# Output projection of the last two chunks split in two, and two expert matrices loaded at other times

## Chip, cores and metric

One core of one Trainium2 chip runs the whole program. The metric is the time of one execution in microseconds of device time (us), as the median of several runs. TensorE (PE) multiplies matrices into PSUM, VectorE (DVE), ScalarE (ACT) and GpSimd (POOL) work on rows, and SyncE (SP) issues most transfers (DMA) and computes nothing.

## What is computed

The reference is one layer of a streaming encoder for 560 tokens of width 1024 (16 meta tokens, 512 of a prompt, 32 of running streams), all in float32. The parts that matter here:

```
h = rmsnorm(x, g_mix); proj = h @ w_in                       # GLU halves, q, k, v
a_out = silu(layernorm(causal_dwconv(u_hist, conv_w, conv_b)))   # group A, 512 channels
b_out = head_rmsnorm(stick_breaking(q, k_all, v_all, q_start))   # group B, 512 channels
x = x + jnp.concatenate([a_out, b_out], axis=-1) @ w_out     # w_out is 1024 x 1024
x = x + hier_moe(rmsnorm(x, g_ffn), ...)                     # top 2 of 32 experts per token
...
gu = hf @ w_e_in[e]                                          # 1024 x 512 for each expert
act = silu(gu[:, :256]) * gu[:, 256:]
out = out + gates[:, e:e + 1] * (act @ w_e_out[e])           # 256 x 1024 for each expert
```

The weights of the 32 experts are 32 times 2 MB (`w_e_in`) and 32 times 1 MB (`w_e_out`).

## The kernel before

Tokens are held in five chunks: four of 128 rows and a last one of 64 (`ROWS`). The engines' programs are written out by hand, each in a fixed order, and meet at semaphores (`wait_ge`, `then_inc`); nothing is scheduled by a tool.

**First half.** Input projection, convolution, attention. Their outputs stand in `mixt`: `k` 0 to 3 is the convolution's half of the channels, `k` 4 to 7 is attention's. `w_out` lies in the tile `cw` (all 8192 columns; columns 4096 to 8191 are its rows for `k` 4 to 7).

**The middle**, which the change touches. For each chunk `c`, PE's `project(c, ks, ns)` multiplies `mixt` by `wout` into the PSUM banks `OUT_BANK[c]`; `LATE` is the order (4, 5, 6, 7, 0, 1, 2, 3) of `k`. DVE's `residual(c)` waits for `res_done` and adds the result to `x`; ACT and DVE make the second norm (`normed_h2`, `h2_ready`); SP stores it to memory (`h2_dram`) for the experts' gathers; PE turns it (`turn_h2`) and makes the router's scores (`logits`); DVE picks two experts for each token (`choose`, `picks_ready`); PE counts positions (`positions`, which waits for `picks_ready`); DVE and PE make a table of rows (`place_at`, `places`, `entries`, `table`). From that table GpSimd gathers the first rows.

**Last half.** 16 pairs of experts. For a pair `g`, PE runs `gate_up(g)`, `turn(g + 1)`, `turn_act(g)`, `down(g)`. Weights lie in 7 slots for `w_e_in` (`WI_SLOTS`) and 7 for `w_e_out`; expert `e` uses slot `e % 7`. SP loads expert 7 and 8's `w_e_in` only after `gu_done` of pair 0, since they take the slots of experts 0 and 1, expert 7's `w_e_out` after `y_done` of pair 0, and so on: from there each load waits for the slot that PE frees. Slot 6 of `w_e_in` is `cw[:, 4096:8192]`, the place of `w_out`'s second half. Slot 5 is made of pieces of the tile `low` (`wi5`) that hold the second norm's rows and the router's data until the gather.

SP's order around the change is the whole of this:

```
            load_one_wo(1)
            for c in range(NC):
                if c == 4:
                    sp.wait_ge(res_done, NC)
                    load_wi(4)
                sp.wait_ge(h2_ready, c + 1)
                sp.dma_start(h2_dram[...], h2[c % 2][...])
            load_wi(6)
            sp.wait_ge(logit_done, NC)
            ...
            sp.wait_ge(gathered[0], 16)
            load_wi(5)
            load_one_wo(4)
            sp.wait_ge(ent_ready, 1)
            load_one_wo(6)
```

Of the kernel before, what the change touches and what calls it, by code (L numbers as in the profile page):

```python
# [11 lines left out]
ALU = mybir.AluOpType  # L12
# [8 lines left out]
P = 128  # L21
# [3 lines left out]
NI = CC // P  # L25
# [8 lines left out]
ROWS = [P, P, P, P, COLS - 4 * P]  # L34
# [13 lines left out]
WI_SLOTS, WO_SLOTS, ROW_BUFS = 7, 7, 1  # L48
# [17 lines left out]
def build(nc, x_prompt, x_sample, cache_k, cache_v, cache_conv, meta, g_mix, w_in, conv_w, conv_b,  # L66
          ln_g, ln_b, g_sb, w_out, g_ffn, w_rg, b_rg, w_re, b_re, w_ei, w_eo, g_fin,
          y_p, y_s, nk_p, nv_p, ncv_p, nk_s, nv_s, ncv_s):
    with ExitStack() as ctx:
# [9 lines left out]
        x = sb("x", [P, NC, D])  # L79
# [78 lines left out]
        def two(lo):  # L158
# [17 lines left out]

        wi = [t.rearrange("p (k n) -> p k n", k=KD)
              for t in [slots[q][:, 0:4096] for q in (2, 3, 0, 1, 4, 5)] + [cw[:, 4096:8192]]]
        wi5 = [(slice(0, 6), lowf[:, 9216:12288].rearrange("p (k n) -> p k n", k=6)),
               (slice(6, KD), lowf[:, 6144:7168].rearrange("p (k n) -> p k n", k=2))]  # L180

        def wi_at(e, k):

            if e % WI_SLOTS == 5:
                return wi5[k // 6][1][:, k % 6, :]
            return wi[e % WI_SLOTS][:, k, :]

        wo = [t.rearrange("p (k n) -> p k n", k=2)
# [255 lines left out]
            return CHUNK_OF.index(c) + 1  # L444

        OUT_BANK = (4, 2, 6, 2, 6)
        MEAN_BANK, LN_BANK = 2, 0

        acc = ps[:, 6:8, :].rearrange("p b n -> p (b n)")[:, 0:CW]
        shared = [(0, j) for j in range(SHARED_FROM, TAPS)] + [(1, j) for j in range(TAPS)]  # L450
# [33 lines left out]
        def _(sp):  # L484
# [112 lines left out]
            load_wi(1)  # L597
            sp.wait_ge(small_stored, 16 * 8)
            load_one_wo(1)
            for c in range(NC):  # L600
                if c == 4:
                    sp.wait_ge(res_done, NC)
                    load_wi(4)
                sp.wait_ge(h2_ready, c + 1)
                sp.dma_start(h2_dram[P * c:P * c + ROWS[c], :], h2[c % 2][0:ROWS[c], :]).then_inc(h2_stored[c % 2], 16)
            load_wi(6)
            sp.wait_ge(logit_done, NC)
            sp.wait_ge(h2_stored[0], 16 * 3)
            sp.wait_ge(h2_stored[1], 16 * 2)
            sp.wait_ge(gsub_ready, 3)  # L610
            sp.wait_ge(gathered[0], 16)
            load_wi(5)
            load_one_wo(4)
            sp.wait_ge(ent_ready, 1)
            load_one_wo(6)
# [259 lines left out]
        def _(pe):  # L875
# [266 lines left out]

            LATE = (4, 5, 6, 7, 0, 1, 2, 3)

            def project(c, ks, ns=(0, 1)):
                w = ROWS[c]

                def ready(k):
                    if k < NI and c == 0:
                        pe.wait_ge(mixa_ready, k + 1)  # L1150
                    elif k == NI:
                        pe.wait_ge(mixb_ready, mixed(c))

                if w < P:
                    for k in ks:
                        for n in ns:
                            mm = pe.matmul(ps[w * n:w * n + w, OUT_BANK[c] + n, :], mixt[:, k, P * c:P * c + w],
                                           wout[:, k, 512 * n:512 * n + 512], start=k == LATE[0], stop=k == LATE[-1],
                                           skip_group_check=True)
                    mm.then_inc(res_done, 1)  # L1160
                    return
                for n in ns:
                    for k in ks:
                        if n == ns[0]:
                            ready(k)
                        mm = pe.matmul(ps[0:w, OUT_BANK[c] + n, :], mixt[:, k, P * c:P * c + w],  # L1166
                                       wout[:, k, 512 * n:512 * n + 512], start=k == LATE[0], stop=k == LATE[-1],
                                       skip_group_check=True)
                if ks[-1] == LATE[-1] and ns[-1] == 1:
                    mm.then_inc(res_done, 1)  # L1170
# [36 lines left out]
            def turn_h2(c):  # L1207
                w = ROWS[c]
                pe.wait_ge(h2_ready, c + 1)
                if c >= 1:  # L1210
                    pe.wait_ge(h2t_ready, c)
                else:
                    pe.wait_ge(co_ready, 2)
                pt = ps[:, 0:2, :].rearrange("p b (k t) -> p (b k) t", t=P)
                for k in range(KD):
                    mm = pe.transpose(pt[:, k, 0:w], h2[c % 2][0:w, P * k:P * k + P], ident[0:w, 0:w])
                    if c == NC - 1 and k == KD // 2 - 1:
                        mm.then_inc(h2_turned, 1)
                mm.then_inc(h2_turned, 1)

            def logits(c):

                if c == 0:
                    pe.wait_ge(router_loaded, 16 * 5)
                if c >= 2:
                    pe.wait_ge(at_ready, c - 1)
                w = ROWS[c]
                pe.wait_ge(h2t_ready, c + 1)
                for k in range(KD):
                    if c == NC - 1 and k == KD // 2:  # L1230
                        pe.wait_ge(h2t_ready, NC + 1)
                    mm = pe.matmul(ps[0:w, 4 + c % 2, 0:36], h2t[c % 2][:, k, 0:w], wrt[:, k, :],
                                   start=k == 0, stop=k == KD - 1, skip_group_check=True)
                mm.then_inc(logit_done, 1)
# [51 lines left out]

            turn_co()
            project(0, LATE[4:])
            project(1, LATE[4:])
            turn_h2(0)  # L1290
            project(2, LATE[4:], (0,))
# [2 lines left out]
            turn_h2(1)  # L1294
            project(2, LATE[4:], (1,))
            logits(1)
            project(3, LATE, (0,))
            turn_h2(2)
            positions(0)
            project(3, LATE, (1,))  # L1300
            positions(1)
            logits(2)
            pe.wait_ge(x2_ready, 3)
            project(4, LATE)
            turn_h2(3)
            positions(2)
            pe.wait_ge(x2_ready, 4)
# [23 lines left out]

            def gate_up(g):
                for e in (2 * g, 2 * g + 1):
                    pe.wait_ge(wi_loaded[e % WI_SLOTS], (e // WI_SLOTS * 16 + 16) * (2 if e % WI_SLOTS == 5 else 1))
                pe.wait_ge(xt_ready, g + 1)
                if g == 2:
                    pe.wait_ge(tab_ready, 2)
# [402 lines left out]
        def _(dve):  # L1740
# [3 lines left out]
            def halves(t):  # L1744
                return t.rearrange("p (a t) -> p a t", a=2)
# [300 lines left out]
            def residual(c):  # L2046

                w = ROWS[c]
                dve.wait_ge(res_done, c + 1)
                if w == P:  # L2050
                    dve.tensor_tensor(x[0:w, c, :].rearrange("p (a n) -> p a n", a=2), x[0:w, c, :].rearrange("p (a n) -> p a n", a=2),
                                      ps[0:w, OUT_BANK[c]:OUT_BANK[c] + 2, :], ALU.add).then_inc(x2_ready, 1)
                else:
                    for n in range(2):
                        cols = slice(512 * n, 512 * n + 512)
                        dve.tensor_tensor(x[0:w, c, cols], x[0:w, c, cols], ps[w * n:w * n + w, OUT_BANK[c] + n, :], ALU.add).then_inc(x2_ready, 1)

            def normed_h2(c):
# [23 lines left out]
                rooted[0] += 1  # L2082
                dve.wait_ge(rstd_ready, rooted[0])
                dve.tensor_scalar(h, h, stat[0:w, 32 + c:33 + c], None, ALU.mult).then_inc(h2_ready, 1)

            def choose(c):

# [51 lines left out]
            link(dve.tensor_scalar(low2.rearrange("p c k f -> p c (k f)"), wide(colid, 4), -BIGF, None, ALU.add))  # L2139
            link(dve.tensor_scalar(low2[:, :, 1, 1], low2[:, :, 1, 1], float(COLS), None, ALU.add))  # L2140
            normed_h2(0)
            residual(1)
            normed_h2(1)
            residual(2)
# [195 lines left out]
```

## Time and profile before

| | |
|---|---|
| median of 3 runs | 561.22 us (561.11 to 561.43) |
| the profiled execution's own time | 562.51 us |
| its span, first to last instruction | 560.8 us |
| PE busy | 507.7 us (91%) |
| DVE, ACT, POOL busy | 267.4, 165.8, 146.3 us |
| mean granted TensorE clock | 0.97 |
| moved by DMA | 148.93 MB, mean 266 GB/s |

The profile is of one execution. Its own time is 1.7 us more than its span (what lies before the first and after the last instruction) and 1.3 us over the median. PE is busy in most of the span, but a share over the whole span says little here: the DMA engines move 420 GB/s in the last 40% of the span and 2 GB/s in some stretches before it.

### The profile page before, as it was taken

Reading aid. Unit: us, or ns where it says so; the run is one execution under the profiler, and the core shown is the slowest. Engines: PE = TensorE matmul, PEld = TensorE weight load, DVE = VectorE, ACT = ScalarE, POOL = GpSimd, SP = SyncE. Lnnn points to the kernel's source line nnn. Section 1 sums busy time; section 2 is a strip of 40 time slices with the busy share of each in tenths; the row PEclk is TensorE's granted clock in tenths of the full one; section 3 lists DMA queues with packets and bytes.
Section 4 is the critical chain, followed back from the end, with each engine's and each line's share of the span. In section 5 each row is a group of like instructions: output and inputs, shape, how many; then the busy total and the mean of one; then the engine's idle time right before and its main releaser. Section 6 shows DMA issues by size and latency. Waiting matters only on the chain.

```text
span 560.8 us, 7885 instructions
## 1 busy us (share of the span) xinstructions
PE 507.7 (91%) x3147; PEld 320.5 (57%) x3148; DVE 267.4 (48%) x471; ACT 165.8 (30%) x280; POOL 146.3 (26%) x143
## 2 busy tenths in 40 slices
PE   5999999999979889999997999999999678798993
PEld 5679999999847567545556634344434223333330
DVE  1870788999578897225668422111111111111157
ACT  4422555554476784032112011111111110111122
POOL 3002699998210102101021202111211110111003
PEclk9999999999979999999996899999999998999997
DMA  8902855500523602599117799999999999999994
GB/s 290 246 12 61 279 158 175 195 0 1 196 76 122 226 1 49 203 429 406 58 56 302 272 415 425 421 428 419 422 421 420 425 426 424 423 418 421 393 345 164
DMA packets 44763, 148.93 MB, mean 266 GB/s; under 512 B 7124, under 2 KB 23532, under 8 KB 36279
## 3 DMA queue, kind: packets, MB, share of 16 engines
q1 hardware_dynamic: 40263, 139.63, 64.3%
q0 software_dynamic: 4464, 8.80, 4.2%
q8 instruction: 25, 0.41, 0.3%
q14 instruction: 11, 0.09, 0.1%
HBM read 136.29 MB, written 19.59 MB: 278 GB/s over the span
## 4 chain that ended last, share of the span: by engine, by line
PE 61%; DMA 20%; DVE 9%; issue 4%; SPq 4%; ACT 1%; POOL 1%; DVEq 0%; POOLq 0%; ACTq 0%
PE ps L949 18%; DMA big<-in_w_expert_out 13%; PE ps L1166 10%; PE ps L1348 9%; PE ps L1373 5%; DMA cw<-h_dram,low 4%; PE ps L914 3%; DVE ps L1928 3%; SPq L628 2%; PE ps L1069 2%; PE ps L1329 2%; DMA y_dram<-cw,low 1%; PE ps L1017 1%; DMA big<-y_dram 1%; PE ps L902 1%
## 5 line engine op out<-in xcount | busy, mean ns | idle before, releaser
L2230 DVE TENSOR_TENSOR low<-low,ps 128x256 f32<-128x256 f32 x16 | 6.7, 422 | 173.2 <-ACT low L1700 173.2
L1348 PE MATMUL ps<-big,low 128*64 128x512 f32 x320 | 85.0, 593 | 3.7 <-issue 2.3
L949 PE MATMUL ps<-cw_r 128*128 128x280 f32 x256 | 72.3, 292 | 0.0
L949 PE MATMUL ps<-low_r,cw_r 128*128 128x280 f32 x256 | 72.2, 292 | 0.0
L949 PE MATMUL ps<-cw_r,big_r 128*128 128x280 f32 x256 | 72.1, 291 | 0.0
L1851 DVE SCALAR_TENSOR_TENSOR ps<-low,cwt,ps 128x590 f32<-128x590 f32 x80 | 66.9, 837 | 2.8
L1373 PE MATMUL ps<-big,low 128*64 128x512 f32 x160 | 46.9, 629 | 11.5 <-DMA big<-in_w_expert_out 4.6
L1166 PE MATMUL ps<-cw,low 128*128 128x512 f32 x128 | 56.6, 595 | 0.0
L1348 PEld LDWEIGHTS ps<-big,low 128*64 128x64 f32 x320 | 29.8, 137 | 46.0 <-issue 45.9
L734 POOL TENSOR_TENSOR big<-big 128x590 f32<-128x590 f32 x36 | 46.9, 1304 | 3.3
L949 PEld LDWEIGHTS ps<-cw_r 128*128 128x128 f32 x256 | 47.2, 188 | 0.4 <-issue 0.4
L949 PEld LDWEIGHTS ps<-cw_r,big_r 128*128 128x128 f32 x256 | 47.3, 188 | 0.0
L949 PEld LDWEIGHTS ps<-low_r,cw_r 128*128 128x128 f32 x256 | 47.2, 188 | 0.0
L1711 ACT ACTIVATE cw<-ps,low 128x1024 f32<-128x1024 f32 x16 | 17.8, 1115 | 98.1 <-PE ps L1373 98.1
L1348 PE MATMUL ps<-low 128*64 128x512 f32 x128 | 42.3, 593 | 0.2 <-issue 0.2
L814 POOL DMA_INDIRECT y_dram<-cw,low x15 | 15.1, 1009 | 101.7 <-ACT cw L1711 96.6
L802 POOL DMA_INDIRECT cw<-h_dram,low x16 | 16.6, 1035 | 94.1 <-PE ps L1329 82.5
L1166 PEld LDWEIGHTS ps<-cw,low 128*128 128x128 f32 x128 | 23.7, 190 | 26.8 <-issue 26.8
L1700 ACT ACTIVATE low<-ps 128x256 f32<-128x256 f32 x16 | 6.2, 384 | 108.5 <-PE ps L1348 108.5
L712 POOL TENSOR_TENSOR stat<-stat,nhalf 128x1 f32<-128x1 f32 (+2 forms) x16 | 15.3, 957 | 83.9 <-DVE stat L2075 32.6
L724 POOL TENSOR_TENSOR big_r<-big,cw_r 128x1024 fp32r<-128x1024 f32 x13 | 31.2, 2400 | 11.6 <-ACT cw_r L1494 11.6
L1373 PEld LDWEIGHTS ps<-big,low 128*64 128x64 f32 x160 | 14.8, 144 | 31.3 <-issue 31.3
(274 smaller groups left out, 816.7 us busy)
## 6 DMA issues: line engine op xcount, KB each, us to landing
big<-in_w_expert_in SPq DMA_DIRECT2D x16, 2048.0 KB, 20.6
big<-in_w_expert_out SPq DMA_DIRECT2D x20, 1024.0 KB, 26.1
big<-in_w_in SPq DMA_DIRECT2D x20, 512.0 KB, 5.3
low<-in_w_expert_out SPq DMA_DIRECT2D x8, 1024.0 KB, 31.5
low<-in_w_expert_in SPq DMA_DIRECT2D x4, 2048.0 KB, 23.3
cw<-in_w_expert_in SPq DMA_DIRECT2D x4, 2048.0 KB, 27.2
low<-in_w_expert_in SPq DMA_DIRECT2D x4, 1536.0 KB, 22.5
big<-in_w_expert_in SPq DMA_DIRECT2D x6, 1024.0 KB, 32.4
```

What stands on the lines that cost most here:

```text
L712: pool.tensor_tensor(t, t, nhalf[0:t.shape[0], :].broadcast_to(list(t.shape)), ALU.pow).then_inc(rstd_ready, 1)
L724: pool.tensor_tensor(w_lo[j % WSLOTS], win[j % WSLOTS], w_hi[j % HSLOTS].bitcast(F32), ALU.subtract).then_inc(w_lo_ready, 1)
L734: pool.tensor_tensor(conv[:, i, :], t, conv[:, i, :], ALU.add).then_inc(pool_tap_done, 1)
L802: pool.indirect_dma_start(out=xg_of(g), out_offset=None, in_=h2_dram, in_offset=bass.IndirectOffsetOnAxis(ap=rows_of[:, g, 0:1].bitcast(U3 ...
L914: mm = pe.matmul(ps[:, 4 + c % 2, :], h[:, k, cols], wts[:, k, :], start=m == 0 and k == 0, stop=m == 2 and k == KD - 1, skip_group_check= ...
L949: return pe.matmul(ps[:, proj_bank(j) + half, 0:PROJ], w[:, k, :], h[:, k, cols], start=first, stop=last, skip_group_check=True)
L1166: mm = pe.matmul(ps[0:w, OUT_BANK[c] + n, :], mixt[:, k, P * c:P * c + w], wout[:, k, 512 * n:512 * n + 512], start=k == LATE[0], stop=k = ...
L1348: mm = pe.matmul(ps[TILE * half:TILE * half + TILE, gu_bank(g), :], xt[:, k, TILE * half:TILE * half + TILE], wi_at(2 * g + half, k), star ...
L1373: mm = pe.matmul(ps[TILE * half:TILE * half + TILE, 4 + m, :], gact_t[:, k, TILE * half:TILE * half + TILE], wo[(2 * g + half) % WO_SLOTS] ...
L1711: act.activation((yg_end if g == PAIRS - 1 else yg[b]).rearrange("p (m n) -> p m n", m=2), ps[:, 4:6, :], ACT.Copy, scale=tab[:, g, 2:3]). ...
L1851: ins = dve.scalar_tensor_tensor(acc, src, w, acc, ALU.mult, ALU.add)
L1928: dve.tensor_tensor_scan(k, k, nones[:, 0:1].broadcast_to([P, n]), carry[:, a:a + 1] if cached else 1.0, ALU.mult, ALU.max).then_inc(left_ ...
```

## The change

PE gets `project_late(c)` for chunks 3 and 4. It multiplies attention's half (`k` 4 to 7) of these chunks into other banks (`LATE_BANK`), right behind chunk 0's projection; DVE's `residual_late(c)` adds that to `x`, and the later `project(3)` and `project(4)` take `k` 0 to 3 alone. The second half of `w_out` is then read for the last time much earlier in PE's order, and SP issues expert 6's `w_e_in` into its place before the stores of the second norm, where it stood behind them. `wi5` becomes three pieces; two of them (6 of 8 `k`, 1.5 MB) are loaded as soon as the router's scores and the stores are done, and the third where the whole stood, behind the gather.

```
-        wi5 = [(slice(0, 6), lowf[:, 9216:12288].rearrange("p (k n) -> p k n", k=6)),
+        wi5 = [(slice(0, 4), lowf[:, 9216:11264].rearrange("p (k n) -> p k n", k=4)),
+               (slice(4, 6), lowf[:, 11264:12288].rearrange("p (k n) -> p k n", k=2)),
                (slice(6, KD), lowf[:, 6144:7168].rearrange("p (k n) -> p k n", k=2))]
...
-        MEAN_BANK, LN_BANK = 2, 0
+        MEAN_BANK, LN_BANK, LATE_BANK = 2, 0, {3: 0, 4: 4}
...
             load_one_wo(1)
+            sp.wait_ge(mean_done, 3)
+            load_wi(6)
             for c in range(NC):
...
-            load_wi(6)
             sp.wait_ge(logit_done, NC)
             sp.wait_ge(h2_stored[0], 16 * 3)
             sp.wait_ge(h2_stored[1], 16 * 2)
+
+            def load_first_wi5(n):
+                ks, dst = wi5[n]
+                sp.dma_start(dst, w_ei[0, 5].rearrange("(p k) n -> p k n", p=P)[:, ks]).then_inc(wi_loaded[5], 16)
+
+            load_first_wi5(0)
+            load_first_wi5(2)
             sp.wait_ge(gsub_ready, 3)
             sp.wait_ge(gathered[0], 16)
-            load_wi(5)
+            load_first_wi5(1)
             load_one_wo(4)
...
+            def project_late(c):
+
+                w = ROWS[c]
+                if c == 3:
+                    pe.wait_ge(co_ready, 2)
+                else:
+                    pe.wait_ge(x2_ready, 1)
+                for k in LATE[0:4]:
+                    for n in range(2):
+                        lo = w * n if w < P else 0
+                        mm = pe.matmul(ps[lo:lo + w, LATE_BANK[c] + n, :], mixt[:, k, P * c:P * c + w], wout[:, k, 512 * n:512 * n + 512],
+                                       start=k == LATE[0], stop=k == LATE[3], skip_group_check=True)
+                mm.then_inc(mean_done, 1)
...
-                    pe.wait_ge(co_ready, 2)
+                    pe.wait_ge(dev_ready, NI + 1)
...
             project(0, LATE[4:])
+            project_late(3)
+            project_late(4)
             project(1, LATE[4:])
...
-            project(3, LATE, (0,))
+            project(3, LATE[4:], (0,))
             turn_h2(2)
             positions(0)
-            project(3, LATE, (1,))
+            project(3, LATE[4:], (1,))
...
-            project(4, LATE)
+            project(4, LATE[4:])
...
+            def residual_late(c):
+
+                w = ROWS[c]
+                dve.wait_ge(mean_done, c - 1)
+                if w == P:
+                    dve.tensor_tensor(halves(x[0:w, c, :]), halves(x[0:w, c, :]), ps[0:w, LATE_BANK[c]:LATE_BANK[c] + 2, :],
+                                      ALU.add).then_inc(dev_ready, 1)
+                    return
...
             normed_h2(0)
+            residual_late(3)
+            residual_late(4)
             residual(1)
```

PE, from the projection of chunk 0 on (L1166 and in the changed file L1190 are `project` for whole chunks, L1216 and L1240 `turn_h2`, L1232 and L1257 `logits`). Before:

```order
L1139 MATMUL ps<-ident,low 30x128 x8
L1166 MATMUL ps<-cw,low 128x512 x16
L1216 MATMUL ps<-ident,low 128x128 x8
L1166 MATMUL ps<-cw,low 128x512 x4
L1232 MATMUL ps<-low 128x36 x8
```

The same place of the change:

```order
L1149 MATMUL ps<-ident,low 30x128 x8
L1190 MATMUL ps<-cw,low 128x512 x8
L1165 MATMUL ps<-cw,low 128x512 x8
L1165 MATMUL ps<-cw,low 64x512 x8
L1190 MATMUL ps<-cw,low 128x512 x8
L1240 MATMUL ps<-ident,low 128x128 x8
L1190 MATMUL ps<-cw,low 128x512 x4
L1257 MATMUL ps<-low 128x36 x8
```

Sixteen matmuls (L1165, eight of 128 rows and eight of 64) now stand between chunk 0's and chunk 1's projection.

PE, from the scores of chunk 1 to those of chunk 2 and the projection of chunk 4 (L1242 and L1267 are `positions`, L1157 and L1181 `project` of the chunk of 64 rows). Before:

```order
L1232 MATMUL ps<-low 128x36 x8
L1166 MATMUL ps<-cw,low 128x512 x8
L1216 MATMUL ps<-ident,low 128x128 x8
L1242 MATMUL ps<-low,tril 128x32
L1166 MATMUL ps<-cw,low 128x512 x8
L1242 MATMUL ps<-low,onesb 128x32
L1242 MATMUL ps<-low,tril 128x32
L1232 MATMUL ps<-low 128x36 x8
L1157 MATMUL ps<-cw,low 64x512 x16
L1216 MATMUL ps<-ident,low 128x128 x8
```

The same place of the change:

```order
L1257 MATMUL ps<-low 128x36 x8
L1190 MATMUL ps<-cw,low 128x512 x4
L1240 MATMUL ps<-ident,low 128x128 x8
L1267 MATMUL ps<-low,tril 128x32
L1190 MATMUL ps<-cw,low 128x512 x4
L1267 MATMUL ps<-low,onesb 128x32
L1267 MATMUL ps<-low,tril 128x32
L1257 MATMUL ps<-low 128x36 x8
L1181 MATMUL ps<-cw,low 64x512 x8
L1240 MATMUL ps<-ident,low 128x128 x8
```

The order is the same, with half as many matmuls ahead of `turn_h2(2)`, ahead of the end of chunk 3 and in chunk 4.

SP, from expert 1's `w_e_out` to the loads behind the gather, with what each waits for (L576 and L578 load a whole `w_e_in`, L574 and L616 pieces of expert 5's, L581 and L583 a `w_e_out`, L605 and L609 store the second norm). Before:

```order
L581 DMA big<-in_w_expert_out 128x2048 [waits small_stored]
L605 DMA h_dram<-low 128x1024 [waits h2_ready] x4
L576 DMA low<-in_w_expert_in 128x4096 [waits res_done]
L605 DMA h_dram<-low 64x1024 [waits h2_ready]
L576 DMA cw<-in_w_expert_in 128x4096
L574 DMA low<-in_w_expert_in 128x3072 [waits gsub_ready,h2_stored1,gathered0,h2_stored0,logit_done]
L574 DMA low<-in_w_expert_in 128x1024
L581 DMA low<-in_w_expert_out 128x2048
```

The same place of the change:

```order
L583 DMA big<-in_w_expert_out 128x2048 [waits small_stored]
L578 DMA cw<-in_w_expert_in 128x4096 [waits mean_done]
L609 DMA h_dram<-low 128x1024 [waits h2_ready] x4
L578 DMA low<-in_w_expert_in 128x4096 [waits res_done]
L609 DMA h_dram<-low 64x1024 [waits h2_ready]
L616 DMA low<-in_w_expert_in 128x2048 [waits h2_stored1,h2_stored0,logit_done]
L616 DMA low<-in_w_expert_in 128x1024
L616 DMA low<-in_w_expert_in 128x1024 [waits gathered0,gsub_ready]
L583 DMA low<-in_w_expert_out 128x2048
```

The load into `cw` (2 MB) has moved ahead of the five stores, and two of the three pieces of expert 5 (1.5 MB) stand ahead of the wait for the gather.

## Rows read from the trace of the kernel before

**Rows 1.** Windows: us, busy of each engine, PE clock, DMA share, GB/s.

```profile
270.00:280.00 10.00, 10.00 (x31) 4.92 (x30) 6.62 (x30) 1.01 (x1) 1.27 (x1) 1.00 0.13 52
280.00:290.00 10.00, 10.00 (x49) 4.95 (x49) 5.43 (x13) 1.15 (x2) 1.33 (x1) 1.00 0.01 2
308.00:310.00 2.00, 2.00 (x12) 2.00 (x11) 1.73 (x11) 0.70 (x1) 1.40 (x2) 0.50 0.01 4
311.90:322.00 10.10, 10.10 (x86) 5.43 (x86) 4.96 (x20) 0.00 (x0) 0.99 (x1) 0.99 0.90 335
322.00:531.00 209.00, 184.48 (x875) 76.49 (x875) 30.43 (x46) 22.48 (x30) 29.02 (x29) 0.98 1.01 421
```

**Rows 2.** Timeline of PE: start, us, line, records (two for a matmul).

```profile
242.91 13.90 PE L1166 MATMUL ps<-cw,low 128*128 128x512 f32 x32
257.52 3.60 PE L1166 MATMUL ps<-cw,low 128*128 128x512 f32 x8
260.96 1.87 PE L1232 MATMUL ps<-low 128*128 128x36 f32 x16
...
268.71 7.11 PE L1166 MATMUL ps<-cw,low 128*128 128x512 f32 x16
275.66 1.04 PE L1216 MATMUL ps<-ident,low 128*128 128x128 f32 x8
276.53 0.18 PE L1242 MATMUL ps<-low,tril 128*128 128x32 bf16 x1
...
285.45 7.09 PE L1157 MATMUL ps<-cw,low 128*64 128x512 f32 x32
292.47 1.09 PE L1216 MATMUL ps<-ident,low 128*128 128x128 f32 x8
```

**Rows 3.** Timeline of DVE, in brackets idle before and its releaser.

```profile
271.38 0.75 DVE L2084 TENSOR_SCALAR low<-low,stat 128x1024 f32<-128x1024 f32 x1 [0.52 <-POOL stat L712]
...
274.46 0.19 DVE L2104 TENSOR_TENSOR low<-negs 128x32 bf16<-128x32 f32 x1
...
283.78 1.22 DVE L2051 TENSOR_TENSOR x<-x,ps 128x1024 f32<-128x1024 f32 x1 [5.85 <-PE ps L1166]
...
291.68 0.19 DVE L2104 TENSOR_TENSOR low<-negs 128x32 bf16<-128x32 f32 x1
292.58 1.40 DVE L2056 TENSOR_TENSOR x<-x,ps 64x512 f32<-64x512 f32 x2 [0.71 <-PE ps L1157]
```

**Rows 4.** Timeline of SP: its DMA issues.

```profile
298.41 0.59 SPq L576 DMA_DIRECT2D cw<-in_w_expert_in  x1
311.88 0.80 SPq L574 DMA_DIRECT2D low<-in_w_expert_in  x2
312.72 0.43 SPq L581 DMA_DIRECT2D low<-in_w_expert_out  x1
319.29 0.33 SPq L581 DMA_DIRECT2D cw<-in_w_expert_out  x1
322.00 0.80 SPq L576 DMA_DIRECT2D big<-in_w_expert_in  x2
327.74 0.33 SPq L581 DMA_DIRECT2D big<-in_w_expert_out  x1
```

**Rows 5.** DMA issues at 292.58 and 319.29, us to landing; the page's software queue.

```profile
low<-in_w_expert_in SPq DMA_DIRECT2D x1, 2048.0 KB, 7.8
...
cw<-in_w_expert_out SPq DMA_DIRECT2D x1, 1024.0 KB, 7.7
...
q0 software_dynamic: 4464, 8.80, 4.2%
```

**Rows 6.** Windows of PE alone: us, busy, clock, DMA share, GB/s.

```profile
298.00:300.00 2.00, 1.70 (x19) 0.62 0.91 356
162.00:164.00 2.00, 1.18 (x16) 0.50 0.00 0
190.00:192.00 2.00, 0.78 (x4) 1.00 0.52 198
```

More of the change, by code:

```diff
@@ L184, in wi_at @@
             if e % WI_SLOTS == 5:
-                return wi5[k // 6][1][:, k % 6, :]
+                ks, t = wi5[(0, 0, 0, 0, 1, 1, 2, 2)[k]]
+                return t[:, k - ks.start, :]
             return wi[e % WI_SLOTS][:, k, :]
@@ L1143, in _ @@
             LATE = (4, 5, 6, 7, 0, 1, 2, 3)
+            def project_late(c):
[10 more added lines that the diff above has]
+                mm.then_inc(mean_done, 1)
             def project(c, ks, ns=(0, 1)):
-                w = ROWS[c]
+                w, first = ROWS[c], LATE[0 if c < 3 else 4]
                 def ready(k):
@@ L1157, in project @@
                             mm = pe.matmul(ps[w * n:w * n + w, OUT_BANK[c] + n, :], mixt[:, k, P * c:P * c + w],
-                                           wout[:, k, 512 * n:512 * n + 512], start=k == LATE[0], stop=k == LATE[-1],
+                                           wout[:, k, 512 * n:512 * n + 512], start=k == first, stop=k == LATE[-1],
                                            skip_group_check=True)
@@ L1166, in project @@
                         mm = pe.matmul(ps[0:w, OUT_BANK[c] + n, :], mixt[:, k, P * c:P * c + w],
-                                       wout[:, k, 512 * n:512 * n + 512], start=k == LATE[0], stop=k == LATE[-1],
+                                       wout[:, k, 512 * n:512 * n + 512], start=k == first, stop=k == LATE[-1],
                                        skip_group_check=True)
@@ L1224, in logits @@
                     pe.wait_ge(router_loaded, 16 * 5)
+                    pe.wait_ge(dev_ready, NI + 3)
                 if c >= 2:
@@ L1333, in gate_up @@
                 for e in (2 * g, 2 * g + 1):
-                    pe.wait_ge(wi_loaded[e % WI_SLOTS], (e // WI_SLOTS * 16 + 16) * (2 if e % WI_SLOTS == 5 else 1))
+                    pe.wait_ge(wi_loaded[e % WI_SLOTS], (e // WI_SLOTS * 16 + 16) * (len(wi5) if e % WI_SLOTS == 5 else 1))
                 pe.wait_ge(xt_ready, g + 1)
@@ L2050, in residual @@
                 if w == P:
+                    if c == 3:
+                        dve.wait_ge(dev_ready, NI + 1)
                     dve.tensor_tensor(x[0:w, c, :].rearrange("p (a n) -> p a n", a=2), x[0:w, c, :].rearrange("p (a n) -> p a n", a=2),
@@ L2053, in residual @@
                 else:
+                    dve.wait_ge(dev_ready, NI + 3)
                     for n in range(2):
@@ L2084, in normed_h2 @@
                 dve.tensor_scalar(h, h, stat[0:w, 32 + c:33 + c], None, ALU.mult).then_inc(h2_ready, 1)
+            def residual_late(c):
[5 more added lines that the diff above has]
+                    return
+                for n in range(2):
+                    cols = slice(512 * n, 512 * n + 512)
+                    dve.tensor_tensor(x[0:w, c, cols], x[0:w, c, cols], ps[w * n:w * n + w, LATE_BANK[c] + n, :],
+                                      ALU.add).then_inc(dev_ready, 1)
             def choose(c):
```

## The prediction

> **What bounds the kernel now.** I read the windows first, to find where the DMA engines work and where they rest. In 270 to 290 they move 52 and 2 GB/s, in 308 to 310 they move 4, and from 322 to 531 they hold 421 GB/s at a busy share of 1.01 [rows 1]. So the last half is bound by the weights: in those 209 us PE is busy 184.5, and it is PE that waits. The middle is another matter. There I read PE's timeline: from 242.91 to 293.56 (the end of the turn that starts at 292.47) PE has no pause, projection after projection [rows 2]. DVE waits for PE (5.85 us ahead of chunk 3's residual, 0.71 us ahead of chunk 4's) [rows 3]. From chunk 4's residual at 292.58 a chain of short steps leads to the table, to the gather, landed when SP passes its wait at 311.88, and to `gu_done` of pair 0 at 322.00 [rows 3, 4].
>
> SP's timeline shows what links the two. The loads of the experts 7 and 8 are issued at 322.00 because the slots come free then, the next `w_e_out` at 327.74 when PE frees one [rows 4]. All 14 slots have been filled or are on their way by 322. So the end of the kernel is: the time of pair 0's `gu_done`, plus what is still to be moved at that moment, over 421 GB/s, plus a tail. A load that is made earlier helps only by what is still queued at 322.
>
> **The queue at 322, which the change can take away.** From 311.88 to 319.29 SP issues 2.10 MB (expert 5's `w_e_in`), 1.05 and 1.05 MB [rows 4] (2048 and 1024 KB are 2.097 and 1.049 million bytes). In 311.9 to 322, 10.1 us at 335 GB/s move 3.38 MB [rows 1]. Left: 0.81 MB, and up to 0.28 of gathers besides (8.80 MB of the software queue over 31 gathers and scatters [rows 5]): 1.9 to 2.6 us at 421. A second way: in 322 to 531 it moves 209 x 421 = 88.0 MB [rows 1]; issued after 322 are 25 experts of 3.146 MB (78.6), 28 gathers or scatters (8.0) and the last gain vector (0.5), together 87.1; left 0.9 MB or 2.1 us. A third: the 1 MB issued at 319.29 lands 7.7 us later, at 327.0; the 2 MB issued at 292.58 into an idle queue took 7.8 [rows 5], of which 5.0 are bytes, so 2.8 are fixed; the queue at 322 is 327.0 - 322.0 - 2.8 = 2.2 us. I take 2.2. With the change 1.57 MB of the 4.19 are gone before the gather. What is left at the gather (0.52 + 1.05 MB, 3.7 us) is over before the wait for `ent_ready`, 7.4 us after it [rows 4], and the last 1.05 MB takes 2.5 us against the 2.7 to the next issue. So the queue is empty at `gu_done`: **gain 2.2 us** (1.9 to 2.6), and not the 3.67 MB / 421 = 8.7 us of what was moved. Expert 6's 2 MB counts nothing: before, issued at 298.41, it was through by the window 308 to 310 already [rows 1, 4]. Behind `gu_done` the stream is just fed: 4.19 MB last 10.0 us, the 1.05 MB issued 5.7 us after them follow at once, then a gather and a scatter, 13.8 us in all against 12.6 us to the next pair's issue.
>
> **The PE order, which costs.** `project_late` moves work, it adds none. Eight matmuls of 128 rows are 16 records, 268.71 to 275.66, or 6.95 us. Chunk 4's 32 records last 7.02 (285.45 to 292.47), and half of them 3.51 [rows 2]. So everything on PE behind chunk 0's projection comes **10.5 us later** at first: PE has no pause there in which to hide it. Their own waits (for the copy of `turn_co`, for residual 0) end before PE comes, since 6.9 us of projection lie between. `residual_late` on DVE, 1.22 and 1.40 us by its twins [rows 3], falls into DVE's wait for chunk 1, which is 10.5 us longer.
>
> The 10.5 us should come back when the second halves are shorter. Step by step, at old times plus 10.5 in brackets where it matters:
> - `project(3)`'s first part starts at 268.71 and now lasts 3.44 (8 records, 257.52 to 260.96 [rows 2]) in place of 6.95: 272.15. The normed rows of chunk 2 are there at 271.38 + 0.75 = 272.13 [rows 3], so `turn_h2(2)` starts at 272.2 and lasts 0.87 [rows 2]: 273.1. Given back: 3.5.
> - `positions(0)` stands next and waits for `choose(0)`, whose last instruction ends at 274.46 + 0.19 = 274.65 [rows 3]. Before, PE came to it at 276.53 and found it done [rows 2]. Now PE waits **1.6 us**, and with it the second part of `project(3)`, which starts at 274.9 and ends at 278.3 (shown by DVE as 283.78 before): 5.4 earlier than before, less 10.5, that is 5.1 later.
> - DVE's chain behind it is unchanged: residual 3, a place, the norm, `choose(2)`, from 283.78 to 291.87 [rows 3], 8.1 us. Before, PE's long `project(4)` covered it and DVE still waited 0.71 us. Now `project(4)` is 3.5 us shorter and ends before this chain, so **DVE is what is late**: residual 4 starts at 291.9 + 5.1 = 297.0, not 292.58. That is **4.5 us later**; only 6.0 of the 10.5 come back. (Bounds: 2.9 if the 1.6 us wait were absent; the wait moves nothing else.)
> - From residual 4 to the gather every step follows as before, since `logits(3)` waits for ScalarE's copy, which its order puts behind chunk 4's squares, and those behind residual 4. So the gather and `gu_done` are 4.5 us later too.
>
> **Small ones.** SP's new wait for `mean_done` ends near 260.4, and the first store is queued behind it and behind 2 MB: its buffer is written again some 18 us later, so nothing waits. Expert 4's load goes with `res_done`, about 2 us later, with pairs to spare. The pieces ahead of the gather take 3.7 us of an idle DMA, and the gather is issued 7 us behind them: nothing. The third piece of `wi5` costs SP 0.4 us four times (0.80 for two issues [rows 4]), in a queue that is full: 0, at most 1.6.
>
> **Sum.** 560.8 + 4.5 - 2.2 = 563.1 of span, 562.5 + 2.3 = 564.8 for the profiled execution's own time; that one stands 1.3 over the median, so the forecast in the median is 561.2 + 2.3 = **563.5 us**, 0.4% slower. Its own range is 562.2 to 564.8 (the bounds of the queue, a third of the wait's doubt, and part of the pieces).
>
> **Rivals.**
> 1. *The early bytes count in full.* The last half is bound by DMA, and 3.67 MB go into idle time [rows 1]; 8.7 - 4.5 = 4.2 us faster, 557.0. It decides if loads beyond the 14 slots can start before `gu_done`. Against it are the issues at 322.00 and 327.74, bound to slots [rows 4]. This is what "Rules for kernel authors" in the Trainium skill's page DMA: Bandwidth & Descriptors would advise, to issue a transfer early and wait for it late; the trace agrees that there is idle time, and shows no free slot. Chance 0.08.
> 2. *The order costs nothing* (the other side): the 10.5 us come back whole, because the chain of `choose` and the norm is shorter than I take it where PE does not crowd it. Then the queue's 2.2 us are all: 559.0. It decides when residual 4 starts under 294.8. For it: PE's total is unchanged. Against it: DVE had only 0.71 us to spare [rows 3]. Chance 0.12.
> 3. *In between*: half of the delay, 2.2 us, against the queue's 2.2: 561.2. Chance 0.20.
> 4. *The queue gives nothing*, because the stream behind `gu_done`, fed with 1.2 us to spare, breaks once: 561.2 + 4.5 = 565.7. Chance 0.07.
> 5. *The clock falls.* PE's new pauses of 1.6 us (at `positions(0)`) and some 1.5 (at `positions(2)`) come close together. After two 2 us windows with little work the clock was 0.50, in 162 to 164, and it fell to 0.62 in 298 to 300; with 0.78 us of work in 190 to 192 it stayed at 1.00 [rows 6]. The nearest row to one pause is the last, so I take 1.00. If it fell, the second part of `project(3)` would take 3.4 us more: 566.9. "HAM oscillation — how this bites in real kernels" in the Trainium skill's page TensorE: Matmul & The Clock Gate warns of such waits between groups of matmuls; the rows bear it out for the longer stretch alone. Chance 0.07.
>
> My own case has 0.46. The range leaves out rivals 1 and 5 and reaches from rival 2 to a little over 4: 559.0 to 566.0. Within 0.2% (1.1 us, about what a measurement of this kernel can tell from no change) lie rival 3 and little else: 0.20. Faster: rivals 1 and 2, 0.20. Slower: 0.60.
>
> **What would show it.** In the changed profile: `project_late` (L1165) near 250 to 260 without a pause; PE idle 1.5 us ahead of `positions(0)`, released by DVE's `choose`; no idle time of DVE ahead of chunk 4's residual, which starts near 297; the gather passed near 316.4 and the next pair's loads issued near 326.5; DMA idle in 272 to 294, and again for some us between the gather and `ent_ready`, which before it was not; the `w_e_out` issued at `ent_ready` landing in 5.5 us, not 7.7. The prediction is wrong if residual 4 starts by 295, or if `gu_done` is 4 us later and the end is not 2.

## The result

The changed kernel takes **567.43 us** in the median of 4 runs (566.0 to 568.88); the kernel before took 561.33 beside it (561.11 to 561.55, 4 runs). The ratio is 1.0109 with a 95% interval of 1.0082 to 1.0135: 1.1% or 6.1 us slower. The forecast was 563.5 in a range of 559.0 to 566.0: the sign was right, the size was not. The span of the profiled execution grew from 560.8 to 565.8 us, 5.0 us; its own time, 567.63, is close to the median, while that of the kernel before, 562.51, stands 1.2 over its median.

Timeline of PE after the change (start, us, line, records; in brackets the idle time before and its releaser), against [rows 2]:

```profile
249.91 10.61 PE L1165 MATMUL ps<-cw,low 128*128 128x512 f32 x32
...
279.48 3.68 PE L1190 MATMUL ps<-cw,low 128*128 128x512 f32 x8
283.00 1.06 PE L1240 MATMUL ps<-ident,low 128*128 128x128 f32 x8
285.48 0.19 PE L1267 MATMUL ps<-low,tril 128*128 128x32 bf16 x1 [1.43 <-DVE low L2147]
285.52 3.68 PE L1190 MATMUL ps<-cw,low 128*128 128x512 f32 x8
...
290.97 3.65 PE L1181 MATMUL ps<-cw,low 128*64 128x512 f32 x16
294.92 1.09 PE L1240 MATMUL ps<-ident,low 128*128 128x128 f32 x8 [0.29 <-DVE low L2114]
...
301.24 3.60 PE L1257 MATMUL ps<-low 128*128 128x36 f32 x16 [0.46 <-ACT low L1688]
```

The late halves run without a pause from 249.91 to 260.5 and put all behind them 10.5 us back. PE waits 1.43 us ahead of `positions(0)` for `choose(0)`. Further on a thing shows that the sum had set to nothing (rival 5 gave it a chance of 0.07): `logits(3)` (301.24) takes 3.60 us, where the 16 records of an earlier `logits` took 1.87 at 260.96 in [rows 2].

Timeline of DVE at the same place, against [rows 3], and of GpSimd below it:

```profile
282.15 0.75 DVE L2114 TENSOR_SCALAR low<-low,stat 128x1024 f32<-128x1024 f32 x1 [0.52 <-POOL stat L722]
...
289.30 1.22 DVE L2080 TENSOR_TENSOR x<-x,ps 128x1024 f32<-128x1024 f32 x1 [0.59 <-PE ps L1190]
...
295.65 0.98 DVE L2138 TENSOR_SCALAR low<-low 128x4 f32<-128x4 f32 x1
...
297.94 0.19 DVE L2147 TENSOR_TENSOR low<-negs 128x32 bf16<-128x32 f32 x1
298.05 1.39 DVE L2086 TENSOR_TENSOR x<-x,ps 64x512 f32<-64x512 f32 x2
```

```profile
294.70 1.91 POOL L800 MEMSET cw<- 128x2048 f32 x1 [0.70 <-PE ps L1181]
```

Chunk 4's residual starts at 298.05 right behind `choose(2)`, with no idle time: DVE is the late one, as forecast, 5.5 us later than 292.58. One instruction of `choose(2)` on 128 x 4 elements lasts 0.98 us; the same in `choose(1)` lasts 0.23. It stands under GpSimd's memset (which fills a tile with zeros), released at 294.70 and over at 296.61, and ends within 0.02 us of it.

SP and its transfers, against [rows 4, 5], then windows of the whole core (busy time of PE, PEld, DVE, ACT, POOL, clock, DMA share, GB/s) and three of PE alone:

```profile
260.56 0.33 SPq L578 DMA_DIRECT2D cw<-in_w_expert_in  x1
...
307.93 10.84 SPq L616 DMA_DIRECT2D low<-in_w_expert_in  x3
318.82 0.43 SPq L583 DMA_DIRECT2D low<-in_w_expert_out  x1
326.09 0.33 SPq L583 DMA_DIRECT2D cw<-in_w_expert_out  x1
328.81 0.80 SPq L578 DMA_DIRECT2D big<-in_w_expert_in  x2
...
cw<-in_w_expert_out SPq DMA_DIRECT2D x1, 1024.0 KB, 4.8
```

```profile
324.00:326.00 2.00, 2.00 (x12) 0.73 (x10) 1.73 (x9) 0.00 (x0) 0.00 (x0) 1.00 0.52 207
326.00:328.00 2.00, 2.00 (x12) 0.86 (x10) 0.07 (x1) 0.00 (x0) 0.00 (x0) 1.00 0.50 86
```

```profile
296.00:298.00 2.00, 0.01 (x1) 1.00 1.08 348
298.00:300.00 2.00, 1.81 (x13) 0.69 0.98 360
300.00:302.00 2.00, 1.54 (x8) 0.50 1.08 459
```

Pair 0's `gu_done`, at which SP issues the next pair's loads, came at 322.00 and comes at 328.81: **6.8 us later**. The queue is empty ahead of it: 207 and 86 GB/s in 324 to 328, and the `w_e_out` issued at 326.09 lands in 4.8 us where it took 7.7. So of 6.8 us the end gets 5.0 in these two executions, and 1.8 were made up behind `gu_done`. Where, SP's issue of the last stage's reads shows, before and after:

```profile
532.44 5.33 SPq L660 DMA_DIRECT2D big<-y_dram  x10
```

```profile
537.91 5.13 SPq L670 DMA_DIRECT2D big<-y_dram  x10
```

From `gu_done` to it took 210.4 us and takes 209.1: 1.3 us less, in the stretch that waits for the loads. The other 0.5 lie behind it, up to the end of the span (28.4 and 27.9 us), when the last expert load has long been issued. The 6.8 us are 5.5 up to residual 4; 1.1 from there to GpSimd's issue of the gather (16.8 us, 298.05 to 314.86, where it was 15.7); and 0.2 behind it (a stretch that takes 13.1 to 14.0 us in the traces of the new order, so 0.2 is no finding). The granted clock goes with the 1.1: after 296 to 298, in which PE worked 0.01 us, it fell to 0.50 in 300 to 302, its lower level of 1.2 GHz, ahead of `logits(3)`. Before, it fell in 298 to 300, behind `logits(3)` [rows 6] and behind two windows in which PE had worked 1.28 and 1.84 us:

```profile
294.00:296.00 2.00, 1.28 (x13) 1.00 0.79 279
296.00:298.00 2.00, 1.84 (x18) 1.00 0.97 418
```

The experiments' traces agree: from residual 4 to the gather's issue took 16.8 us in the one other in which `logits(3)` met the low clock (e1), and 15.7 in e3, e6, f1, f2, f3 and f4, where it did not.

### The profile page after: what moved, and what is told of

It is laid out like the page before. It is cut to its first block, busy times and chain, and to the rows that moved or that the text cites. A ratio compares the mean times of both kernels' runs of the same rounds, so it can differ in the third digit from the quotient of the medians.

```text
span 565.8 us, 7894 instructions
## 1 busy us (share of the span) xinstructions
PE 511.9 (90%) x3147; PEld 323.6 (57%) x3148; DVE 270.6 (48%) x474; ACT 165.9 (29%) x280; POOL 147.4 (26%) x143
## 4 chain that ended last, share of the span: by engine, by line
PE 58%; DMA 22%; DVE 8%; SPq 5%; issue 3%; ACT 2%; POOL 1%; DVEq 0%; POOLq 0%; ACTq 0%
PE ps L959 18%; DMA big<-in_w_expert_out 12%; PE ps L1190 8%; PE ps L1375 6%; DMA cw<-h_dram,low 6%; PE ps L1400 5%; PE ps L924 3%; SPq L583 2%; DMA big<-y_dram 2%; DVE ps L1955 2%; PE ps L1165 2%; PE ps L1079 2%; PE ps L1356 2%; DMA y_dram<-cw,low 1%; PE ps L1064 1%
## 5 line engine op out<-in xcount | busy, mean ns | idle before, releaser
L1190 PE MATMUL ps<-cw,low 128*128 128x512 f32 x112 | 50.0, 596 | 0.0
L1190 PEld LDWEIGHTS ps<-cw,low 128*128 128x128 f32 x112 | 20.6, 190 | 23.3 <-issue 23.3
```

## The experiments

Twelve kernels ran, in three sets of four; each was timed beside the kernel before (561.46, 561.91 and 562.13 us in the median of the three sets), and the ratio with its 95% interval is to that. The changed kernel itself was in none of the three sets. A median set against its 567.43 us therefore carries the drift of the kernel before between sets, up to 0.8 us; the ratios (1.0109 for the changed kernel) don't.

**Which part costs?** Four kernels take the change apart.

`e1_order_alone`: PE's and DVE's new order, with both loads in their old places.

```
-            sp.wait_ge(mean_done, 3)
-            load_wi(6)
...
+            load_wi(6)
             sp.wait_ge(logit_done, NC)
...
             sp.wait_ge(gathered[0], 16)
+            load_first_wi5(0)
+            load_first_wi5(2)
             load_first_wi5(1)
```

> The changed PE and DVE order alone: expert 6's w_e_in is loaded behind the stores and all of expert 5's behind the gather, as before the change. Theory 1 (the order delays pair 0's gu_done, and only expert 5's early pieces give something back): gu_done at about 328.8 as in the changed kernel, no empty queue between the gather and gu_done, the end some 2 us later than the changed kernel's, so 569 to 570 us in the median. Theory 2 (the moved loads cost something, the stores behind 2 MB or the three pieces): faster than the changed kernel, 563 to 566 us.

Measured: 569.0 us, 1.0127 (1.0111 to 1.0142), 7.1 us over the kernel before; `gu_done` came at 328.37. The order alone costs all of the loss and a little more; the loads cost nothing. (With them the changed kernel is 1.0 us faster by the ratios, but the intervals overlap.) That is as theory 1 had it, and theory 2 falls.

`e6_wi6_early_alone`: the changed kernel with expert 5's pieces all behind the gather.

```
-            load_first_wi5(0)
-            load_first_wi5(2)
...
             sp.wait_ge(gathered[0], 16)
+            load_first_wi5(0)
+            load_first_wi5(2)
             load_first_wi5(1)
```

> The changed order with expert 6's w_e_in early, but all pieces of expert 5's behind the gather. Theory 1 (2 MB moved between two stretches of idle DMA, both over before gu_done, count nothing): the same time as the order alone within 0.3 us, 569 to 570. Full bytes (2.1 MB over 421 GB/s): 5 us faster than the order alone. Theory 2 (the stores behind it cost): slower than the order alone.

Measured: 567.54 us, 1.0107 (1.0091 to 1.0122), 1.5 us faster than the order alone (1.1 by the ratios), and the same as the changed kernel. None of the three values expected fits. But the traces show another difference between the two. First the order alone, then this one, `logits(3)` on PE:

```profile
301.61 3.60 PE L1256 MATMUL ps<-low 128*128 128x36 f32 x16 [1.25 <-ACT low L1687]
```

```profile
300.96 1.95 PE L1257 MATMUL ps<-low 128*128 128x36 f32 x16 [1.37 <-ACT low L1688]
```

The same instruction behind nearly the same pause, once at the lower clock and once at the full one. `gu_done` came at 326.89, 1.5 us earlier than in the order alone, and 1.1 of that lie between residual 4 and the gather's issue (15.7 us for 16.8). So the 1.5 us can't be put down to expert 6's load; from `gu_done` to the issue of the last stage's reads the two traces take 210.8 and 210.4 us, which leaves that load some 0.4 us, by one trace of each.

`e2_pieces_alone`: the kernel before, with only expert 5's pieces ahead of the gather.

```
-            sp.wait_ge(gsub_ready, 3)
-            sp.wait_ge(gathered[0], 16)
-            load_wi(5)
+            load_first_wi5(0)
+            load_first_wi5(2)
+            sp.wait_ge(gsub_ready, 3)
+            sp.wait_ge(gathered[0], 16)
+            load_first_wi5(1)
```

> The kernel before with one edit: expert 5's w_e_in in three pieces, two of them ahead of the gather. Theory 1: gu_done stays at 322.0, the w_e_out issued at 319.3 lands in about 5 us and not 7.7, and the end comes 1.8 to 2.2 us earlier, 559.1 to 559.6 us. Theory 2: the pieces cost more than they give, 561.3 us or more. Full bytes (1.57 MB over 421 GB/s): 3.7 us earlier, 557.6 us.

Measured: 561.14 us, 0.9995 (0.9986 to 1.0004): 0.3 us faster, of the 1.8 to 2.2 expected, and an interval that takes in no change. `gu_done` stayed where it was (321.74), and the queue did run empty before it. Windows of PE in its trace, DMA share and GB/s at the end of the rows:

```profile
318.00:319.00 1.00, 1.00 (x8) 1.00 0.57 221
319.00:320.00 1.00, 1.00 (x8) 1.00 0.02 4
320.00:321.00 1.00, 1.00 (x6) 1.00 0.80 147
```

`e3_filled`: the changed kernel with spare matmuls in PE's pauses.

```
             turn_h2(2)
+            pe.wait_ge(x2_ready, 3)
+            busy(5, 6)
             positions(0)
...
             turn_h2(3)
-            positions(2)
             pe.wait_ge(x2_ready, 4)
             busy(6)
+            positions(2)
+            busy(9)
             logits(3)
```

> The changed kernel with spare matmuls in PE's pauses ahead of positions(0), ahead of positions(2) and ahead of logits(3) (5, none more than the 6 moved forward, and 9), sized to end when the pause ends. Theory 1 with the clock as a part of its own: the granted clock stays at 1.00 until about 304, logits(3) takes 1.95 us and not 3.6, and gu_done and the end come 1.0 to 1.7 us earlier, 565.8 to 566.5 us in the median, with less spread between runs. If the clock costs nothing, or the matmuls do not hold it: 567.4 us, or later by what they block.

Measured: 567.47 us (567.0 to 568.07), 1.0099 (1.0084 to 1.0115). The clock stayed at 1.00 to 304, `logits(3)` took 1.95 us, and the gather was issued 15.7 us behind residual 4 and not 16.8. `gu_done` came at 327.16, 1.65 us earlier than in the changed kernel's trace: 1.1 of that are the clock; residual 4 came 0.3 later, and the stretch behind the gather's issue, which varies from trace to trace, was 0.9 shorter. The median did not move (the ratio is 0.6 us lower, within the intervals), so it may be that most runs of the changed kernel did not meet the low clock there, which is not shown; the runs lie closer together (1.1 us against 2.9), but four of each don't settle that.

**How the order costs.** `f2_memset_later` holds GpSimd's memset back.

```
                     pool.wait_ge(res_done, NC)
+                    pool.wait_ge(picks_ready, 3)
                     pool.memset(cw[:, 0:2048], 0.0).then_inc(zero_ready, 1)
```

> The changed kernel with GpSimd's memset of 2048 columns (1.9 us) held back until choose(2) is done, so that it runs beside chunk 4's residual as it did before the change. If that memset is what stretches one small instruction of choose(2) from 0.23 to 0.98 us in all four traces of the new order: that instruction takes 0.23 us again, residual 4 and gu_done come 0.75 us earlier, about 566.7 us in the median against 567.4. If it is something else: the 0.98 us stay.

Measured: 566.16 us (565.12 to 567.05), 1.0072 (1.0058 to 1.0085), 1.3 us under the changed kernel by the medians and 2.1 by the ratios, where 0.75 was expected. The instruction takes 0.23 us again, and residual 4 starts at 296.99 with the memset beside it: 1.06 us earlier, of which 0.31 are an earlier start of the whole stretch in that trace and 0.75 the memset. What the median won beyond that isn't explained; in this trace `logits(3)` ran at the full clock. DVE, then GpSimd:

```profile
295.34 0.23 DVE L2139 TENSOR_SCALAR low<-low 128x4 f32<-128x4 f32 x1
...
296.99 1.39 DVE L2087 TENSOR_TENSOR x<-x,ps 64x512 f32<-64x512 f32 x2
```

```profile
297.19 1.80 POOL L801 MEMSET cw<- 128x2048 f32 x1 [3.50 <-DVE low L2148]
```

`f3_positions_later` takes away PE's wait for `choose(0)`.

```
             turn_h2(2)
-            positions(0)
             project(3, LATE[4:], (1,))
+            positions(0)
             positions(1)
```

> The changed kernel with positions(0) behind the second part of project(3), so that PE does not wait for choose(0) there. As the prediction had it (PE's wait of 1.6 us is a term of the delay): residual 4 comes 1.6 us earlier. Theory 1 as it stands now (DVE's own chain from chunk 2's residual to chunk 4's is the bound, and had only 0.59 us of idle time in it): residual 3 comes 0.6 us earlier and so does residual 4, about 566.8 us in the median.

Measured: 566.98 us (565.9 to 567.27), 1.0085 (1.0071 to 1.0099). Residual 3 starts at 288.79, 0.5 us earlier and not 1.6, with no idle time of DVE ahead of it: DVE's own chain is the bound, not PE's wait. But residual 4 did not follow. DVE and GpSimd:

```profile
288.79 1.22 DVE L2080 TENSOR_TENSOR x<-x,ps 128x1024 f32<-128x1024 f32 x1
...
296.17 1.80 DVE L2144 TENSOR_SCALAR low<-low 128x2 f32<-128x2 uint32 x1
```

```profile
296.14 1.80 POOL L800 MEMSET cw<- 128x2048 f32 x1 [2.63 <-PE ps L1181]
```

The memset, released by PE, fell upon another instruction of `choose(2)`, and that one lasted exactly as long as the memset did, 1.80 us for 2 columns. And the clock fell at 291, behind two pauses of PE of 0.49 and 0.55 us, where the changed kernel's one pause of 1.43 us had not lowered it: `project(4)` took 5.35 us in place of 3.65. The median comes near the 566.8 expected, but by luck: residual 4 came 0.3 us later than in the changed kernel's trace and not 0.6 earlier, and `gu_done` was 0.9 us earlier (327.88) because `logits(3)` ran at the full clock.

`f4_all_three` has the later `positions(0)`, the later memset, and the spare matmuls ahead of `positions(2)` and `logits(3)`.

> The changed kernel with positions(0) later, the memset later, and spare matmuls ahead of positions(2) and logits(3). The terms added up: residual 4 at 296.7 (0.6 and 0.75 earlier), logits(3) at full clock (1.65 where it had fallen): gu_done at 325.8 to 326, and 565.0 to 565.8 us in the median. It should stay slower than the kernel before by over 3 us, since DVE has no idle time left between the residuals of chunks 2 and 4.

Measured: 565.31 us (564.66 to 566.12), 1.0061 (1.0047 to 1.0075). Residual 4 starts at 296.86 and `gu_done` comes at 325.77, both as expected, though the second with some luck: the stretch behind the gather's issue was 13.2 us here and 13.95 in the changed kernel's trace. `project(4)` met the low clock here too (5.35 us), and ended ahead of residual 4 all the same. 3.4 us over the kernel before remain, as expected: from chunk 2's residual to chunk 4's DVE had no idle time to give them back, but for 0.5 us in each norm in which it waits for GpSimd, as before the change.

**What the early loads are worth.** `f1_filled_order_alone` is `e3_filled` with the two loads put back, by the edit of `e1_order_alone`.

> The changed kernel with the spare matmuls of the filled kernel, and with both early loads put back to their old places. Its only difference to the filled kernel (567.5 us) is the loads, with the clock held in both. Theory 1 (a queue of 2.2 us at gu_done is all that early loads can take away): 569.2 to 569.7 us. Theory 3 (the early loads are worth next to nothing, and the 1.5 us between the order alone and the changed kernel are the clock at logits(3)): 567.5 to 568.0 us.

Measured: 568.23 us (567.26 to 569.89, 4 runs), 1.0104 (1.0089 to 1.012). Against the filled kernel's ratio of 1.0099 that is 0.3 us (0.8 by the medians), with intervals of 0.9 us to either side. It is nearer to theory 3, but the runs of this one spread too far to decide.

So I measured the queue by itself. `g3_pair0_later` is the kernel before with pair 0's work on PE begun later, its loads and gathers as they were.

```
-            busy(WARM)
+            busy(WARM + 19)
```

> The kernel before with 19 more spare matmuls ahead of pair 0's first turn on PE: gathers and loads as they were, pair 0's gu_done some 5 us later, with the queue behind the gather then run empty before it. Theory 1 (a queue of 2.2 us at gu_done is what can be taken away): the end comes 5.0 - 2.2 = 2.8 us later. Theory 3 (the queue is worth about 1 us or less, since the stream behind gu_done is fed too thinly at first to use an earlier start): 4.0 to 5.0 us later. If gu_done did not set the end: no change.

Measured: 565.08 us, 1.0053 (1.0039 to 1.0066). `gu_done` came at 325.66: 3.7 us later, not 5. The end came 3.0 us later (2.2 to 3.7). So `gu_done` does set the end, and to let the queue run out gave **0.7 us** (0 to 1.5, `gu_done` being read from one trace of each), not 2.2.

`g4_pieces_pair0_later` adds expert 5's early pieces to that, by the edit of `e2_pieces_alone`.

> The same with expert 5's two pieces ahead of the gather. Under both theories the same time as with the spare matmuls alone, within 0.3 us, since in both the queue is empty when gu_done comes. If the early pieces are worth their bytes: 3.7 us less.

Measured: 564.35 us, 1.0038 (1.0024 to 1.0052); `gu_done` at 325.57. 0.7 us under `g3_pair0_later`, more than the 0.3 expected, with ratio intervals that overlap; not the 3.7 of its bytes.

`g1_pieces_no_wo6` leaves the last load ahead of `gu_done` out of `e2_pieces_alone`.

```
-            load_one_wo(6)
+            sp.dma_start(wo[6][:, 0:1, 0:16], ...[:, 0:1, 0:16]).then_inc(wo_loaded[6], 16)
```

> The kernel with expert 5's early pieces alone, and expert 6's w_e_out (1 MB, the last load ahead of gu_done) left out but for a few bytes, so expert 6's result is wrong in it. If what is moved before gu_done costs nothing once the queue is empty there: as with the pieces alone, 0 to 0.6 us less than that (561.1 and 0.3 under the kernel before). If every byte counts: 2.5 us less.

Measured: 561.58 us, 0.9983 (0.997 to 0.9996): by the ratio 1.0 us under the kernel before of its set, 0.7 less than the pieces alone in theirs, where 0 to 0.6 was expected. A megabyte less before `gu_done`, nothing like 2.5 us.

`g2_expert9_not_loaded` leaves 2 MB out behind it.

```
+                elif e == 9:
+                    sp.dma_start(wi[2][:, 0:1, 0:16], rows[:, 0:1, 0:16]).then_inc(wi_loaded[2], 16)
```

> The kernel before with expert 9's w_e_in (2 MB, issued 12.6 us after pair 0's gu_done) left out but for a few bytes, so expert 9's result is wrong in it. If bytes behind gu_done set the end one by one: 2.1 MB over 421 GB/s, 5.0 us faster, 556.5 to 557 us. If PE or the slots set it: less than 2.5 us.

Measured: 557.94 us, 0.9924 (0.9911 to 0.9936), 4.3 us faster (3.6 to 5.0). Bytes behind `gu_done` are paid for nearly in full, bytes before it hardly at all.

Where a part of the queue's 2.2 us went, windows of the 25 us behind `gu_done` show, in this order: the kernel before, the changed one, the pieces alone, pair 0 later (PE busy, clock, DMA share, GB/s):

```profile
322.00:347.00 25.00, 23.56 (x116) 1.00 1.01 420
```

```profile
328.81:353.81 25.00, 23.56 (x116) 1.00 1.01 406
```

```profile
321.74:346.74 25.00, 23.56 (x116) 1.00 1.01 412
```

```profile
325.66:350.66 25.00, 23.56 (x116) 1.00 1.00 406
```

Later all run at 420 to 422 GB/s. These streams from an empty queue move 8 to 14 GB/s less than the kernel before for 25 us: 0.2 to 0.35 MB, or 0.5 to 0.8 us given back. (The other traces spread wider: 399 to 412 GB/s from an empty queue, 415 to 427 from one that still held loads, without g1, which had nothing at all under way and moved 383.) With that the queue is worth 1.4 to 1.7 us by the traces; the medians say 0.3 to 0.7.

A second reading needs no rate. From `gu_done` to the issue of the last stage's reads took 210.4 to 210.8 us in the four traces with loads still queued at `gu_done` (the kernel before, e1, e6, f1), and 208.5 to 209.6 us in eight of the nine in which the queue had run empty (e3, the ninth, took 210.4; g2 moves fewer bytes and is left out). By their medians that is 1.3 us. From there to the end of the span the traces take 27.9 to 30.0 us for the same work, so single traces, and the 1.8 us of the first pair, say less than this stretch.

## Why the prediction was wrong

Two terms of the sum were mis-sized. The order's delay of `gu_done`, put at 4.5 us, was 6.8 in the changed kernel's trace, and the order alone (e1) cost 7.1 us in the median; the memset (0.75) and the clock (1.1) are in it and were not in the sum. And the queue's gain, put at 2.2 us, was 1.3 by the traces and 0.3 to 0.7 by the medians. Neither alone takes the time over the range: 563.5 with the delay's 2.3 us more is 565.8, and with the queue's 0.9 to 1.9 besides it is 566.7 to 567.7, where 567.43 was measured.

- **What bounds the end.** Right. "The time of pair 0's `gu_done`, plus what is still to be moved" held in g1, g2 and g3, and the 3.67 MB moved earlier were worth 0.3 to 1.3 us and not 8.7. Rival 1, the bytes in full, is out.
- **PE's order, 10.5 us back and 6.0 returned.** Right step by step: PE's wait at `positions(0)` was 1.43 us for 1.6, DVE's idle time ahead of chunk 4's residual was gone. Without the memset residual 4 would start at 297.3 for 297.0; 0.13 of that is a later start of the whole stretch in that trace.
- **The bound of 2.9 us for that term.** Wrong. I took PE's wait for a part of the delay; f3 took it away and won 0.5 us up to residual 3. Behind it stood DVE's chain, which I had priced only from residual 3 on and not from residual 2.
- **A term that was missing: the memset, 0.75 us.** I had written that "DVE's chain behind it is unchanged", `choose(2)` with it. GpSimd's memset is released by `res_done` of chunk 4, which came earlier against DVE than before; it used to run beside residual 4 and now runs beside `choose(2)`. f2 and f3 show the cause: the stretched instruction goes where the memset goes.
- **The clock.** I took 1.00 and gave its fall 0.07, and looked for it at `project(3)`. It fell later, ahead of `logits(3)`, in two of the three traces that have the changed PE order and its pauses up to there (changed kernel and e1; not e6; f2 stayed at the full clock too, but with a pause of 1.42 us ahead of `positions(2)` for their 2.18), and at `project(4)` in f3 and f4. In the changed kernel's trace it costs 1.1 us up to the gather. Against the row that I took as nearest, 190 to 192, stands the fall in 298 to 300 [rows 6]: ahead of it PE had worked 1.28 and 1.84 us of two windows of 2, so before the change already the clock fell behind pauses shorter than the new ones, and the chance was set too low. How many of the timed runs met it is not known, since only one of each was traced.
- **The queue, -2.2 us: the second term that failed.** "So the queue is empty at `gu_done`" was right; that this is a gain of all its 2.2 us was not. Between the two profiled executions 1.8 were made up, of which 1.3 are the queue's by the stretch up to the last stage; the medians say 0.3 (e2) and 0.7 (g3). I had written that the stream behind `gu_done` is "just fed"; it is not quite, which by the windows gave 0.5 to 0.8 us back. That is in the direction of rival 4, though no break shows: the lowest microsecond of the changed kernel's 25 still moved 295 GB/s. The rest, up to about 1 us between traces and medians, I can't place: the traced execution of the kernel before is one of its slower ones, and the queue is read from it.

The sum with the measured terms: 4.7 to residual 4 with the trace's late start, 0.75 for the memset, 0 to 1.1 for the clock, 0.2 behind the gather, less 0.3 to 1.3: 4.4 to 6.5 us, against 6.1 measured (4.6 to 7.6). What stays open is how those 2 us share out between clock and queue, and with them the queue's true worth.

No version beats the kernel before: the best of the new order is 3.4 us slower, and the pieces alone, 0.9995, are not to be told from it.

## What to carry to other kernels

When loads are bound to slots, a transfer made earlier gains only what would still be queued when the next slot comes free, less what the stream loses by starting empty; look up that moment first and price the delay of it, since here 3.67 MB moved early gave 0.3 to 1.3 us, and the order that went with them cost 6.8 us of delay to that moment. Work moved forward on a busy engine takes the cover from every chain that it used to hide, so follow the other engine's chain from its first step behind the move, with its idle time as the account. And list what third engines do at a release that has moved: a fill that nobody waits for can still fall upon the critical one.

## What the runs showed of the hardware

- A memset on GpSimd (128 x 2048, 1.80 to 1.92 us) stops a small tensor-scalar instruction on VectorE that starts under it until it ends: 0.98 us for 0.23 in the traces of the changed kernel, e1, e6, e3 and f1, 1.80 us for 0.23 in f3, where both end within 0.03 us of each other. Other small instructions of `choose(2)` started under it too, scalar-tensor-tensor and reduce, and kept their 0.16 to 0.23 us. The Trainium skill's page SBUF — State Buffer, section "Who interferes with whom", says that VectorE in a two-port mode and GpSimd take a shared port pair as an exclusive lock and that the later one blocks fully; the traces agree with a full block. That these instructions ran in such a mode, no run here shows.
- `logits(3)`, 16 records of 128 x 36, took 3.60 us at the lower clock and 1.87 to 1.95 at the full one; `logits(4)`, with weights of 64 columns, took 1.89 at the lower one (changed kernel) and 1.09 at the full one (e3, f4). The falls seen here come behind pauses of PE, but not behind the same pause in each run: with the same PE program and the same pauses to within 0.1 us up to the end of `positions(2)`, the clock fell ahead of `logits(3)` in the changed kernel and e1, and behind it in e6. Nor does the length of one pause decide: 1.43 us alone left the clock at 1.00, and 0.49 and 0.55 us close together were followed by 0.50 (f3).
- The stream of expert loads ran at 420 to 422 GB/s once it was long under way, and at 399 to 412 in the first 25 us from an empty queue (415 to 427 where loads were still queued), with the DMA share at 1.00 to 1.02 in all of them: the busy share doesn't show the difference, the GB/s do.
